# Attention in the mixer: the values stand in the array and the turned probabilities stream past them; its norm from squares summed by TensorE; the output weight's rows in another order

## The reference

```
h = rms_norm(x, g_mix);  gq, gk, gv, gr, ga, sq, sk, sv = split(h @ w_in)
o_gla = chunked gated linear attention, 4 heads of 64 x 128
s = q k^T / 8 + bias(dist), windows of 128 keys and the 128 before;  m = max(max(s), sink)
p = exp(s - m);  p = p / (sum(p) + exp(sink - m));  o_swa = p @ v      # 8 heads, 2 kv heads of 64
o = concat(rms_norm(o_gla, g_gla) * silu(gr), rms_norm(o_swa over its 512 columns, g_swa)) @ w_out
x = x + o
logits = rms_norm(x, g_ffn) @ w_router + b;  top 4 of 32 experts, gates = softmax of the 4
y = sum over the 4 of gate * (clamped_swiglu(h2 @ w_up[e] + b_up[e]) @ w_down[e] + b_down[e])
out = rms_norm(x + y, g_final)
```

## Time and profile before

| | |
|---|---|
| median of 3 runs | 1338.68 us (1337.06 to 1339.67) |
| profiled execution: span, first to last instruction | 1337.8 us |
| its own time beside the span | not listed apart; the median lies 0.9 us above the span |
| PE busy | 1283.2 us, 96% |
| DVE, ACT, POOL busy | 918.0, 285.1, 124.1 us |
| DMA | 468.95 MB, mean 351 GB/s, about 420 GB/s in the expert stage |
| granted TensorE clock | mean 0.995 |
| chain that ended last | PE 71%, DMA 21%, DVE 4% |

### The profile page before, as it was taken

The page is one execution under the profiler, slowest core; times in us unless marked ns, Lnnn a source line. Parts: engine busy times, 40 slices in busy tenths (PEclk is TensorE's granted clock), DMA queues, the critical chain, the costliest instruction groups (busy, mean ns, idle before and its releaser), DMA issues.

```text
span 1337.8 us, 21359 instructions
## 1 busy us (share of the span) xinstructions
PE 1283.2 (96%) x6323; PEld 520.2 (39%) x6323; DVE 918.0 (69%) x1877; ACT 285.1 (21%) x542; POOL 124.1 (9%) x229
## 2 busy tenths in 40 slices
PE   8999999999999999997999998899999997999996
PEld 6876565553333333332333332233333331333332
DVE  3215357656878777775787786687777875777778
ACT  4331143433112121111121121111121111121114
POOL 2000000000020110100110101010111100110100
PEclk9998999999999999999999999999999999999999
DMA  9405154078999999999999999999999999999996
GB/s 358 129 4 191 32 176 170 32 284 342 417 386 386 421 421 419 416 421 421 420 398 423 414 422 420 414 422 407 420 417 420 414 421 421 421 402 420 412 414 274
DMA packets 91409, 468.95 MB, mean 351 GB/s; under 512 B 11870, under 2 KB 29520, under 8 KB 41074
## 3 DMA queue, kind: packets, MB, share of 16 engines
q1 hardware_dynamic: 75070, 441.56, 81.2%
q0 software_dynamic: 7360, 16.79, 3.2%
q10 hardware_dynamic: 8948, 10.19, 2.2%
HBM read 614.82 MB, written 28.77 MB: 481 GB/s over the span
## 4 chain that ended last, share of the span: by engine, by line
PE 71%; DMA 21%; DVE 4%; SPq 2%; issue 1%; ACT 0%; DVEq 0%; POOL 0%; POOLq 0%; ACTq 0%
PE ps L2159 34%; DMA raw<-in_w_down_dram 19%; PE ps L2284 17%; PE ps L1845 5%; PE ps L1822 5%; PE ps L2060 3%; SPq L614 1%; DMA raw<-slot_outputs 1%; PE ps L2173 1%; DVE v_gate L1756 1%; DMA x_rows<-expert_inputs,row_idx 1%; PE ps L1924 0%; PE ps L2007 0%; PE ps L2015 0%; PE ps L2014 0%
## 5 line engine op out<-in xcount | busy, mean ns | idle before, releaser
L2159 PE MATMUL ps<-raw,xT 128*64 128x512 f32 x2816 | 617.4, 593 | 17.6 <-DMA raw<-in_w_up_dram 17.0
L1632 DVE STREAM_TRANSPOSE xT<-x_hold 32x192 f32<-32x192 f32 (+2 forms) x680 | 275.0, 404 | 154.1 <-PE ps L2159 133.9
L2159 PEld LDWEIGHTS ps<-raw,xT 128*64 128x64 f32 x2816 | 199.9, 137 | 424.6 <-issue 391.0
L2284 PE MATMUL ps<-raw,aT 128*64 128x512 f32 x1408 | 317.1, 595 | 16.7 <-DMA raw<-in_w_down_dram 16.7
L1632 DVE STREAM_TRANSPOSE aT<-act_g 32x256 f32<-32x256 f32 x352 | 223.5, 635 | 64.4 <-PE ps L2284 54.5
L2284 PEld LDWEIGHTS ps<-raw,aT 128*64 128x64 f32 x1408 | 97.6, 137 | 229.2 <-issue 174.7
L1016 ACT ACTIVATE act_s<-act_g 128x512 f32<-128x512 f32 x46 | 29.0, 630 | 632.6 <-DVE act_g L1616 632.6
L566 POOL DMA_INDIRECT slot_outputs<-y_rows,out_idx x44 | 45.2, 1028 | 609.3 <-ACT y_rows L1021 608.4
L1404 DVE STREAM_TRANSPOSE bias_up<-up_cols 128x1024 f32<-128x1024 f32 x46 | 57.3, 1245 | 1.6
L1845 PE MATMUL ps<-w_c_cols,hT 128*128 128x512 f32 x128 | 56.8, 596 | 0.0
L558 POOL DMA_INDIRECT x_rows<-expert_inputs,row_idx x47 | 49.3, 1049 | 71.2 <-issue 53.5
(11 more groups left out here) (405 smaller groups left out, 899.7 us busy)
## 6 DMA issues: line engine op xcount, KB each, us to landing
raw<-in_w_up_dram SPq DMA_DIRECT2D x356, 1024.0 KB
raw<-in_w_down_dram SPq DMA_DIRECT2D x180, 1024.0 KB, 10.5
slot_outputs<-zeros ACTq DMA_DIRECT2D x1, 8320.0 KB, 27.9
ahead<-in_w_up_dram SPq DMA_DIRECT2D x8, 1024.0 KB
raw<-slot_outputs SPq DMA_DIRECT2D x8, 1024.0 KB, 16.1
w_c_cols<-in_w_in_dram SPq DMA_DIRECT2D x1, 4096.0 KB, 31.1
w_out_sb<-in_w_out_dram SPq DMA_DIRECT2D x1, 4096.0 KB, 13.8
w_a_cols<-in_w_in_dram SPq DMA_DIRECT2D x1, 2624.0 KB, 12.3
```

Of the source, the lines that this page charges most:

```text
L1632: dve.transpose(dst_at(rows_out, group), src_at(rows_in, parity)).then_inc(done, 1)
L2159: ins = mm(ps[SUB * i:SUB * i + SUB, banks[bank], :], rows_in[:, j, :], weights[:, c:c + HF], start=False, stop=(j == at_end), skip_group_ ...
L2284: ins = mm(ps[SUB * i:SUB * i + SUB, 2, :], aT[:, j, r, :], raw[:, units[j], D * r + HF * i:D * r + HF * i + HF], start=False, stop=(j == ...
```

## The change

Probabilities are now scaled before they are turned: `scale_probs(t)` on DVE multiplies the 128x1024 of each kv head in place, behind `mask_gla(t)` (for tile 1 behind `gla_variance(1)`), and `attend(t)` waits for it instead of for the exponentials. The values stand: for each part and each kv head one product holds 64 columns of `sv` and streams 512 columns of `pT`; the two kv heads write partitions 0-63 and 64-127 of bank 6. The sums so come out turned. ACT's new `take_attention(t)` squares them (`oT_sq`, in `pT`) and copies them with the gain to `oT`. `sum_squares(t)` multiplies the squares by a matrix of ones, so that every partition of bank 5 holds each token's sum; `swa_root(t)` takes the root with 1/512 and epsilon in the same activation, and `make_swa_mix(t)` inverts 128x128 and multiplies straight into `mixT`. Four transposes and `take_mixT` of half 1 go. The head order of the second half of the 1024 columns becomes (head in the group, kv head), so the rows of `w_out` and of `g_swa` are loaded in that order (w_out in three DMAs instead of one, g_swa in two), as are the sample rows. POOL's clearing of `x_rows` waits for a smaller count of `mix_ready`.

```diff
@@ vector: in place of take_attention and swa_variance
-                dve.wait_ge(pv_psum, t)
+            def scale_probs(t):
+                w0 = P - META if t == 1 else 0
+                dve.wait_ge(exp_done, (QH + 1) * t)
                 do(dve.tensor_tensor(soft[:, 0, :], soft[:, 2, :], soft[:, 3, :], ALU.add))
                 do(dve.reciprocal(soft[:, 0, :], soft[:, 0, :]))
                 for g in range(KVH):
-                    step(dve.tensor_tensor(mix[...], ps[:, g, :]..., bc(soft[:, 0, 4 * g:4 * g + 4], 2, [P, 4, HD]), ALU.mult))
+                    of = probs[:, 4 * g:4 * g + 4, w0:2 * P]
+                    dve.tensor_tensor(of, of, bc(soft[:, 0, 4 * g:4 * g + 4], 2, [P, 4, 2 * P - w0]), ALU.mult).then_inc(s_probs, 1)
...
             def make_swa_mix(t):
                 dve.wait_ge(m_root, 2 * t + 1)
-                do(dve.reciprocal(norm[:, 20:21], norm[:, 12:13]))
-                do(dve.tensor_scalar(mix[:, D // 2:D], mix[:, D // 2:D], norm[:, 20:21], None, ALU.mult))
-                dve.sem_inc(mix_ready, 1)
+                do(dve.reciprocal(rstd, rstd))
+                dve.tensor_tensor(mixT[:, GH:KT, :], oT, bc(rstd, 1, [P, 4, P]), ALU.mult).then_inc(mixT_ready, 1)
@@ vector, the loop
             gla_variance(1)
+            scale_probs(1)
             for t in range(PT - 1):
                 residual(t)
                 if t:
                     take_gla(t + 1)
                     gla_variance(t + 1)
-                take_attention(t + 1)
-                swa_variance()
                 make_gla_mix(t + 1)
-                make_swa_mix(t + 1)
                 take_mixT(t + 1, (0,))
                 choose(t)
-                take_mixT(t + 1, (1,))
+                make_swa_mix(t + 1)
                 scores(t + 2)
...
                 mask_gla(t + 2)
+                scale_probs(t + 2)
...
             early_list()
-            swa_variance()
+            make_swa_mix(PT)
             indices(0)
-            make_swa_mix(PT)
-            take_mixT(PT, (1,))
@@ scalar
+            def take_attention(t):
+                act.wait_ge(pv_psum, t)
+                act.activation(oT_sq, ps[:, 6, :].rearrange("p (h q) -> p h q", h=4), ACT.Square)
+                for i in range(4):
+                    ins = act.activation(oT[:, i, :], ps[:, 6, P * i:P * i + P], ACT.Copy, scale=g_outT[:, GH + i:GH + i + 1])
+                ins.then_inc(pv_copied, 1)
...
                 if t < PT:
+                    take_attention(t + 1)
                     gla_roots(t + 1)
-                if t < PT - 1:
-                    swa_root(t + 1)
                 take_h2T(t)
                 take_parts(t)
-                if t == PT - 1:
-                    swa_root(PT)
+                if t < PT:
+                    swa_root(t + 1)
                 gate_powers(t)
@@ tensor, attend(t)
-                pe.wait_ge(exp_done, (QH + 1) * t)
+                pe.wait_ge(s_probs, 2 * t)
                 turn(0)
                 if t == 1:
                     unread(1)
+                pe.wait_ge(s_probs, 2 * t + 1)
                 turn(1)
                 if t == 1:
                     unread(1)
-                weigh(0)
-                weigh(1).then_inc(pv_psum, 1)
+                pe.wait_ge(pT_copied, 4 * t)
+                pe.wait_ge(x2_var, t)
+                for part in range(2):
+                    for g in range(KVH):
+                        ins = mm(ps[HD * g:HD * g + HD, 6, :], sv[:, t - 1 + part, HD * g:HD * g + HD],
+                                 pT[:, 2 * g + part].rearrange("p h q -> p (h q)"), start=(part == 0), stop=(part == 1))
+                ins.then_inc(pv_psum, 1)
+            def sum_squares(t):
+                pe.wait_ge(pv_copied, t)
+                pe.wait_ge(h2T_ready, 2 * t)
+                for i in range(4):
+                    ins = mm(ps[:, 5, 0:P], ones_f[:], oT_sq[:, i, :], start=(i == 0), stop=(i == 3))
+                ins.then_inc(mixT_psum, 1)
@@ tensor, mix_out(t) and last_mix_out()
-                turn_mix(t, 0)
-                turn_mix(t, 1)
+                turn_mix(t)
+                sum_squares(t)
                 sum_parts(t - 1)
@@ gpsimd
-            pool.wait_ge(mix_ready, 2 * PT + 1)
+            pool.wait_ge(mix_ready, PT + 1)
```

More of the change, by code:

```diff
@@ L273, in moe_layer @@
         h2 = B("h2", [P, D])
+        oT, rstd, eps_col = mix[:, D // 2:D].rearrange("p (h q) -> p h q", h=4), mix[:, 0:P], norm[:, 44:45]
+        oT_sq = pT[:, 3]
         g_ffn_bc = B("g_ffn_bc", [P, D])
@@ L787, in _ @@
                 act.dma_start(vec_rows[KT:KT + GH, :], g_gla[0:1, :].to_broadcast([GH, P])).then_inc(ld_gmix, 16)
-                act.dma_start(vec_rows[KT + GH:2 * KT, :], g_swa[0].rearrange("(k p) -> k p", p=P)).then_inc(ld_gmix, 16)
+                for g in range(KVH):
+                    act.dma_start(vec_rows[KT + GH:2 * KT, HD * g:HD * g + HD],
+                                  g_swa[0][4 * HD * g:4 * HD * g + 4 * HD].rearrange("(h x) -> h x", x=HD)).then_inc(ld_gmix, 16)
                 act.dma_start(vec_rows[2 * KT:NVEC, :], b_a[0].rearrange("(k p) -> k p", p=P)).then_inc(ld_gmix, 16)
@@ L857, in gla_roots @@
             def gla_roots(t):
-                act.wait_ge(m_var, 2 * t)
+                act.wait_ge(m_var, t + 1)
                 act.activation(norm[:, 8:12], norm[:, 0:4], ACT.Sqrt).then_inc(m_root, 1)
             def swa_root(t):
-                act.wait_ge(m_var, 2 * t + 1)
-                act.activation(norm[:, 12:13], norm[:, 4:5], ACT.Sqrt).then_inc(m_root, 1)
+                act.wait_ge(mixT_psum, 2 * t + 2)
+                act.activation(rstd, ps[:, 5, 0:P], ACT.Sqrt, scale=1.0 / (QH * HD), bias=eps_col).then_inc(m_root, 1)
+            def take_attention(t):
[4 more added lines that the diff above has]
+                ins.then_inc(pv_copied, 1)
             def roots_ahead():
@@ L1458, in _ @@
             step(dve.tensor_reduce(sum_ident[:], ident[:].rearrange("p (i e) -> p e i", e=NE), AX, ALU.add))
+            step(dve.memset(eps_col, EPS))
             take_mixT(0, (0, 1))
@@ L2008, in turn @@
                         ins.then_inc(pT_psum, 1)
-                def weigh(g):
-                    pe.wait_ge(pT_copied, 4 * (t - 1) + 2 * g + 2)
-                    for i in range(4):
-                        dst = ps[:, g, P * i:P * i + P]
-                        mm(dst, pT[:, 2 * g, i, :], sv[:, t - 1, :], start=True, stop=False)
-                        ins = mm(dst, pT[:, 2 * g + 1, i, :], sv[:, t, :], start=False, stop=True)
-                    return ins
-                pe.wait_ge(exp_done, (QH + 1) * t)
+                pe.wait_ge(s_probs, 2 * t)
                 turn(0)
@@ L2075, in out @@
                               stop=(k == KT - 1))
+                sum_squares(PT)
                 sum_parts(PT - 1)
```

45 lines of the change are left out of this document (17 added, 28 removed).

## The result

The changed kernel takes 1342.88 us (median of 7 runs, 1340.81 to 1344.68) against 1338.65 (7 runs, 1337.06 to 1340.54): ratio 1.0031, 95% interval 1.002 to 1.0042, **slower by 4.2 us**. A second set of 9 runs gave 1343.13 and 1.003 (1.002 to 1.004). I forecast 1340.7 with 1338.0 to 1345.0.

A forecast was written before the change was run, and what follows sets the result against it. The expert stage was taken as bound by its weight stream, the tile loop by TensorE's work; +2.4 (tile 1) - 1.2 (two middle turns) + 0.8 (tile 4) = +2.0 us on 1338.68 gave 1340.7 us, range 1338.0 to 1345.0.

The forecast's parts named there:

- the likeliest case: Whole kernel, no clock fall priced: +2.0 us to 1340.7 us, given 0.56.
- a falling clock: Rival: tile 1's standstill halves the clock, lengthening what follows by 1.7 to 3.4 us, 1342.4 to 1344.1; chance 0.28.
- the saving that I had too small: Two middle turns of the tile loop, 0.6 us gained in each, 1.2 us together.
- Middle turns: Tile loop between first and last turn: output product starts at 256.8 instead of 257.39, 0.6 us gained a turn.
- the term: Middle turn's weighing: paired products end at 251.12 instead of 251.96, 0.84 us won of 1.70.
- ACT's square and copies: ACT after the attention sums: square 0.55 and four scaled copies 1.3, 1.85 us together.
- Tile 1: First turn, uncovered: transposes wait for scaled probabilities, output product at 203.7 instead of 201.32, 2.4 us lost.
- Standstill: Tile 1: TensorE idle 3.8 us before its transposes, waiting for DVE's scaled probabilities.
- Tile 4: Last turn: ACT's root uncovered, output product 1.9 us late, of which 0.8 us remains lost at the gathered rows.
- the 128x128 reciprocal: DVE's inversion for the attention mix: 0.92 us by extension, 0.3 to 1.2 possible, covered in middle turns.
- The loads: Three more DMAs for `w_out` and `g_swa`: some 0.4 us of issue each, costed at nothing.
- DVE's residual: Middle turns: margin 0.3 us before the residual, yet a slip of up to 2 us still free.

The follow-up runs named there:

- early clear: Kernel before, with POOL clearing `x_rows` as early as in the change and tile 4's attention variance using other scratch: 1338.33 us, 1.0002 to before.
- Early scaling: Changed kernel, tile 1's probabilities scaled ahead of the gated copy and variance, attention sums there waiting for ACT's copies instead of DVE's residual: 1338.53 us.
- Four edits: Changed kernel with tile 1's early scaling, ACT's gated root first, tile 4's row list first, and first value products waiting for three copied quarters: 1337.16 us.
- Fill both: Changed kernel with four unread TensorE products in tile 1's gap and four more in tile 4's gap: 1340.88 us, 1.0019 to the kernel before.
- the split wait: Changed kernel, first pair of value products waiting for three of four copied quarters, second pair for all four; alone 1341.32 us, 1.0017 to before.
- Fill tile 1: Changed kernel with four unread TensorE products in tile 1's gap only: 1340.11 us, 1.0007 to the kernel before.

## Why the prediction was right and where it was wrong

The sign, the places and the range were right; the likeliest case was not what happened. It had the clock at 1.00 and +2.0; measured was +4.2, the side that I had given to a falling clock. That the sum came no further off is partly luck: its terms without the clock should have come to +1.0, and the saving that I had too small stood against the fall that I had left out.

**Middle turns: mechanism right, size off.** Predicted -0.6, measured -1.22. Counted from the output product before, turned `h` now starts 21.76 us behind it (22.60 before), 0.84 earlier, exactly the term. The other 0.6 are rows that I took as work and that held waits: the scores (0.12 less), the router (0.57 instead of the 0.72 of the earlier trace rows), four transposes (0.49, not half of 1.28), and `sum_parts` to the output product (0.14, not 0.36). ACT's square and copies took 1.5 (253.32 to 254.82), not 1.85, so nothing waited for them.

**Tile 1: the step that failed is the clock, put at nothing in the sum.** Standstill 3.88 for my 3.8. Without the clock the loss is 2.0 to 2.15 (22.73 = 25.35 less 2.62; 22.87 with the gap filled), for my 2.4. The fall adds 1.6 to 2.6: I had priced it at 1.7 to 3.4 and given it 0.28, because the products on both sides are 128 wide. Every profile with the 3.9 us gap left open (5 of 5) has the fall, none of those with it filled or removed (7 of 7). The Trainium skill's rule (TensorE: Matmul & The Clock Gate, "Why this matters for your kernels"), that idle gaps between bursts cost the full clock, was the better guide for tile 1, and these profiles agree with it there. Idle gaps do not explain the fall at the outer products, where TensorE was busy throughout (1.00 before).

**Tile 4: right at its start in part, wrong behind it, and the clock again.** The output product came 1.33 late for my 1.9: the root stood 0.3 earlier than I had it, because ACT's square and copies were shorter, and from the transposes to the output product it took 2.30 for my 2.6. I then let 1.1 of the 1.9 come back before the second block. `turn_rows(0)` did come back by 0.56 (285.66 to 300.26 is 14.60, against 15.16 before), most of it the four transposes that left this stretch, but the next block did not: 41.53 us against 41.57, because TensorE waited 0.39 longer for gathered rows (below). The early clear shows the same from the other side, a gather 1.5 us sooner that bought nothing. So +0.8 should have been +1.3. And I did not look for a fall here: with the gap of 2.25 the clock fell in five of six profiles of kernels that had it. It cost 1.45 us in tile 4 of the changed kernel, and some 1.6 with the end of the fall, which reaches into the stretch behind. With 1.95 or less, or filled, it fell in none of eight. The length of the gap alone does not decide it: in tile 1 a gap of 2.17 (Early scaling, Four edits) had no fall in either profile, and in tile 4 one of 2.25 had none in one profile. What decides stays open.

**Costed at nothing and rightly so:** the 128x128 reciprocal took 0.95 us (estimate from the rows 0.92; the 1.2 that I had worked out from the Trainium skill, VectorE: DVE Perf Modes, where the repeat count stands under "First, the fixed hardware budget", is not borne out). The loads moved nothing that the start of tile 0's product shows (180.59 us in Fill both, 180.60 before, both with a fall of 7 us ahead of it). In the middle turns DVE's residual started right behind the scaling and still gave `h` in time.

**Sum with the measured terms:** +2.1 and 1.6 to 2.6 for the clock in tile 1, -2.4 for two turns, +1.3 and up to 1.6 for the clock in tile 4: 2.6 to 5.2, around the measured 4.2. Timed runs have no trace, so how often each fall is in them is not known; what is shown is that the kernels with both gaps removed or shortened are 6 to 8 us faster than the changed one, at least 1.0 of it from the split wait, which has nothing to do with these gaps.

The stretch from tile 4's output product to the second block varied from 41.1 to 43.0 us. In every profile it splits into TensorE's two waits for gathered rows (`x_rows`; 1.1 to 2.7 us together, 1.19 before, 1.58 and 1.71 in the two of the changed kernel, 2.69 with Early scaling) and a rest. The rest is 39.95 us with the changed queue, 40.0 to 40.5 where a fall of the clock in tile 4 reaches into it, and 40.4 to 40.5 with the queue of before, which has four transposes more there. So what varies is how long TensorE waits for the gathered rows; why they land later in some kernels stays open.

## What to carry to other kernels

A change that makes the bounding engine's work shorter (here 1.7 us a turn) must be followed to the first and last turn of the loop, where the cover is thinner: the whole loss sat in tile 1 and tile 4, and reordering DVE's and ACT's steps there, with a finer wait, turned a 0.3% loss into a 0.3% gain (the version with this gain also has two short fillers, whose own worth is not shown). Where rows show the clock falling behind a gap in TensorE, price such a gap at its length plus what follows at half clock, and when you fill one, measure the filler first: four products where two fitted cost as much as the fall. An idle time that a row does not print may still be in its distance to the next row.

## What the runs showed of the hardware

The clock fell in places and not in others from one execution to the next of one kernel: in tile 4 of the changed kernel once in two profiles, and at or just behind the outer products for seven microseconds, for three and a half, or not at all, with tile 0's output product at 180.6 to 182.3, 179.3 to 179.6, or 177.3 to 177.4 us. From the first of the 64 small products to the wide ones behind them that is 9.61 us (before, 107.63 to 117.24), 7.95 (changed, 107.98 to 115.93) or 6.35 (Fill tile 1, 107.62 to 113.97), so the fall alone is worth up to 3.3 us, most of what the whole change costs. Comparing two single profiles by their end would have misled, and only the ledger by stretches told what belonged to the change.
